# Weight buffers 128 bytes longer, and 41 weight panels written and read 32 or 64 bytes further on

## The reference

```python
for i in range(2):
    hn = rmsnorm(h, mix_norm[i])
    h = h + (mixer_ab if i == 0 else mixer_c)(hn, ...)
    u = rmsnorm(h, ffn_norm[i]) @ ffn_up[i]          # 1024 -> 2 x 2816
    gate, up = split(conv3(u) + conv_b)
    h = h + (silu(gate) * up) @ ffn_down[i]          # 2816 -> 1024
    h = h + sigmoid(rmsnorm(h, ple_norm[i]) @ ple_gate[i]) * (p[i] @ ple_proj[i])
```

## Time and profile before

| | |
|---|---|
| time, median of 3 runs | 1003.98 us (1003.67 to 1004.08) |
| time of the profiled execution | 1004.01 us |
| its span, first to last instruction | 1002.1 us |
| PE busy | 984.9 us, 98% |
| PEld busy | 883.2 us, 88% |
| DVE busy | 677.7 us, 68% |
| ACT busy | 573.5 us, 57% |
| granted TensorE clock | 1.000 |

### The profile page before, as it was taken

The page is one execution under the profiler, slowest core; times in us unless marked ns, Lnnn a source line. Parts: engine busy times, 40 slices in busy tenths (PEclk is TensorE's granted clock), DMA queues, the critical chain, the costliest instruction groups (busy, mean ns, idle before and its releaser), DMA issues.

```text
span 1002.1 us, 15515 instructions
## 1 busy us (share of the span) xinstructions
PE 984.9 (98%) x6218; PEld 883.2 (88%) x6218; DVE 677.7 (68%) x969; ACT 573.5 (57%) x801; POOL 133.8 (13%) x116
## 2 busy tenths in 40 slices
PE   8999999999999999999999999999999999999997
PEld 8998889999988888788999998888988889988886
DVE  5787577888864567886788886456564566854555
ACT  7747747656553576785756655356464465534433
POOL 4003202343310000000143331001000000000010
PEclk9999999999999999999999999999999999999999
DMA  9654256686555464336766655546635544466551
GB/s 310 207 170 126 84 146 178 197 250 195 185 195 184 167 210 168 126 103 171 198 172 182 194 172 203 177 166 205 211 127 169 168 149 146 142 197 205 175 172 56
DMA packets 159655, 174.33 MB, mean 174 GB/s; under 512 B 4126, under 2 KB 120336, under 8 KB 159584
## 3 DMA queue, kind: packets, MB, share of 16 engines
q1 hardware_dynamic: 157248, 167.65, 53.3%
q0 software_dynamic: 2160, 5.41, 1.7%
q10 hardware_dynamic: 176, 0.27, 0.1%
HBM read 172.25 MB, written 1.07 MB: 173 GB/s over the span
## 4 chain that ended last, share of the span: by engine, by line
PE 85%; ACT 6%; DVE 5%; issue 2%; DMA 1%; POOL 0%; POOLq 0%; ACTq 0%; DVEq 0%
PE bank L870 32%; PE bank L845 29%; PE bank L902 16%; PE bank L890 2%; ACT w_hi L1215 2%; PE bank L1004 1%; PE bank L930 1%; DVE w_lo L1541 1%; DMA w_raw<-in_ab_w_in 1%; ACT le L1325 1%; ACT L1325 1%; PE bank L950 0%; PE bank L973 0%; DVE le_s L1891 0%; ACT le_s L1465 0%
## 5 line engine op out<-in xcount | busy, mean ns | idle before, releaser
L1541 DVE TENSOR_TENSOR w_lo<-w_raw,w_hi 128x2048 fp32r<-128x2048 f32 x154 | 351.9, 2288 | 186.8 <-ACT w_hi L1215 186.6
L1215 ACT ACTIVATE w_hi<-w_raw 128x2048 fp32r<-128x2048 f32 x155 | 296.2, 1914 | 247.5 <-PE bank L870 114.2
L870 PE MATMUL bank<-x_hi,w_hi 128*128 128x256 f32 x720 | 205.9, 286 | 2.7 <-DVE w_lo L1541 1.8
L870 PE MATMUL bank<-x_lo,w_hi 128*128 128x256 f32 x720 | 203.7, 283 | 0.0
L870 PE MATMUL bank<-x_hi,w_lo 128*128 128x256 f32 x720 | 203.7, 283 | 0.0
L870 PEld LDWEIGHTS bank<-x_hi,w_hi 128*128 128x128 f32 x720 | 138.0, 192 | 4.4 <-DVE w_lo L1541 2.0
L845 PE MATMUL bank<-w_hi,x_hi 128*128 128x512 f32 x352 | 139.8, 397 | 1.0 <-DVE x_lo L1555 0.7
L870 PEld LDWEIGHTS bank<-x_lo,w_hi 128*128 128x128 f32 x720 | 138.1, 192 | 0.2
L870 PEld LDWEIGHTS bank<-x_hi,w_lo 128*128 128x128 f32 x720 | 138.0, 192 | 0.0
L845 PE MATMUL bank<-w_hi,x_lo 128*128 128x512 f32 x352 | 137.3, 390 | 0.0
L845 PE MATMUL bank<-w_lo,x_hi 128*128 128x512 f32 x352 | 137.1, 390 | 0.0
(11 more groups left out here) (344 smaller groups left out, 1471.6 us busy)
## 6 DMA issues: line engine op xcount, KB each, us to landing
w_raw<-in_ffn_up SPq DMA_DIRECT2D x88, 512.0 KB, 5.2
w_raw<-in_w_in SPq DMA_DIRECT2D x35, 1024.0 KB, 5.1
w_raw<-in_ffn_down SPq DMA_DIRECT2D x22, 1024.0 KB, 5.0
w_raw<-in_ab_w_in SPq DMA_DIRECT2D x13, 1024.0 KB, 5.4
w_raw<-in_ple_gate SPq DMA_DIRECT2D x8, 1024.0 KB, 5.1
w_raw<-in_c_w_in SPq DMA_DIRECT2D x6, 1024.0 KB, 5.3
w_raw<-in_ab_w_out SPq DMA_DIRECT2D x4, 1024.0 KB, 5.1
w_raw<-in_w_mem_kv SPq DMA_DIRECT2D x4, 1024.0 KB, 5.1
```

The lines of the kernel that those rows point to most:

```text
L870: mm = pe.matmul(bank[b][:, c * 256:c * 256 + 256], wv[w][:, k, c * P:(c + 1) * P], x[:, k, :], start=(k == 0 and m == 0 and not (first an ...
L1215: act.activation(whi[n % RING][:, :], raw[n % RAW][:, :], ACT.Copy).then_inc(*mark("weights_hi", ("hi", n)))
L1541: dve.tensor_tensor(wlo[n % RING][:, :], raw[n % RAW][:, :], plain(whi[n % RING][:, :]), ALU.subtract).then_inc(*mark("weights_lo", ("lo", ...
```

## The change

The six buffers of `w_hi` and `w_lo` become 32 floats (128 bytes) longer. In the panels of a table `SHIFTED`, the 2048 floats begin 8 or 16 floats (32 or 64 bytes) into the room instead of at its start; in the table the first number is for `w_hi`, the second for `w_lo`. The writers (ACT, DVE, POOL) and the reader (TensorE) all go by it. Everything behind a room moves by 128 bytes for each room ahead of it, `x_hi` and all that follows by 768 bytes. To make space, `causal` loses its own place and is loaded into columns 384 to 639 of `vecs`, which held the convolution's taps.

```diff
+SHIFT = 32
...
+SHIFTED = {}
+for _i in range(4):
+    SHIFTED["down0", _i], SHIFTED["down0", 4 + _i] = (16, 16), (0, 16)
+    SHIFTED["down1", _i], SHIFTED["down1", 4 + _i] = (16, 0), (8, 8)
+    SHIFTED["up1", 2 + _i], SHIFTED["up1", 7 + _i], SHIFTED["up1", 12 + _i], SHIFTED["up1", 17 + _i] = (16, 16), (0, 16), (16, 0), (8, 8)
+for _i in range(3):
+    SHIFTED["up0", 10 + _i], SHIFTED["up0", 14 + _i], SHIFTED["up0", 18 + _i] = (16, 16), (0, 16), (16, 0)
...
-        whi = [fixed(f"w_hi{i}", [P, 2048], F32R) for i in range(RING)]
-        wlo = [fixed(f"w_lo{i}", [P, 2048], F32R) for i in range(RING)]
+        hi_room = [fixed(f"w_hi{i}", [P, 2048 + SHIFT], F32R) for i in range(RING)]
+        lo_room = [fixed(f"w_lo{i}", [P, 2048 + SHIFT], F32R) for i in range(RING)]
+
+        def w_hi(n):
+            a = SHIFTED.get(PANELS[n][:2], (0, 0))[0]
+            return hi_room[n % RING][:, a:a + 2048]
+
+        def w_lo(n):
+            a = SHIFTED.get(PANELS[n][:2], (0, 0))[1]
+            return lo_room[n % RING][:, a:a + 2048]
...
-        causal = r("causal", [P, T])
...
+        causal = vflat[:, 3 * P:3 * P + T]
...
-                    load(causal[:, :], io["c_causal"], "causal")
+                    load(causal, io["c_causal"], "causal")
...
-                wh, wl = whi[n % RING], wlo[n % RING]
+                wh, wl = w_hi(n), w_lo(n)
```

More of the change, by code:

```diff
@@ L737, in _ @@
                     for c in (slice(512 * q, 512 * q + 512) for q in range(4)):
-                        pool.tensor_tensor(wlo[n % RING][:, c], raw[n % RAW][:, c], plain(whi[n % RING][:, c]), ALU.subtract).then_inc(*mark("weights_lo_p", ("lo", n)))
+                        pool.tensor_tensor(w_lo(n)[:, c], raw[n % RAW][:, c], plain(w_hi(n)[:, c]), ALU.subtract).then_inc(*mark("weights_lo_p", ("lo", n)))
                 elif kind == "sb_scores":
@@ L831, in panel @@
                     block, half = where[2:]
-                    wv = [w[:, :].rearrange("p (k n) -> p k n", k=4) for w in (wh, wl)]
+                    wv = [w.rearrange("p (k n) -> p k n", k=4) for w in (wh, wl)]
                     for t in range(TT):
@@ L855, in panel @@
                     claim(b, ("ev", n))
-                    wv = [w[:, :].rearrange("p (k n) -> p k n", k=KT) for w in (wh, wl)]
+                    wv = [w.rearrange("p (k n) -> p k n", k=KT) for w in (wh, wl)]
                     first = i == 0
@@ L883, in panel @@
                                 claim(out_bank(t, half), ("h", stage, t) if down else ("ym", stage[-1], 2 * t + half) if branch else ("ev", FIRST["gate" + stage[-1]] + 2 * half + 1))
-                    wv = [w[:, :].rearrange("p (k n) -> p k n", k=2) for w in (wh, wl)]
+                    wv = [w.rearrange("p (k n) -> p k n", k=2) for w in (wh, wl)]
                     if branch and last:
@@ L1214, in split @@
                         act.wait_ge(*at(("pe", n - RING)))
-                    act.activation(whi[n % RING][:, :], raw[n % RAW][:, :], ACT.Copy).then_inc(*mark("weights_hi", ("hi", n)))
+                    act.activation(w_hi(n), raw[n % RAW][:, :], ACT.Copy).then_inc(*mark("weights_hi", ("hi", n)))
             def split_piece(n, i):
@@ L1220, in split_piece @@
                 act.wait_ge(*at(("raw_half", i // 2) if n == 0 else ("raw", n)))
-                act.activation(whi[n % RING][:, c], raw[n % RAW][:, c], ACT.Copy).then_inc(*mark("weights_hi", ("hi_piece", n, i)))
+                act.activation(w_hi(n)[:, c], raw[n % RAW][:, c], ACT.Copy).then_inc(*mark("weights_hi", ("hi_piece", n, i)))
             act.dma_start(xn[0:2 * KT, 0, 0:P], io["mix_norm"].rearrange("l (a c) -> (l a) c", c=P)).then_inc(*mark("load_mix_gain", ("loaded", "mix_gain"), by=16))
@@ L1540, in split @@
                     dve.wait_ge(*at(("hi", n)))
-                    dve.tensor_tensor(wlo[n % RING][:, :], raw[n % RAW][:, :], plain(whi[n % RING][:, :]), ALU.subtract).then_inc(*mark("weights_lo", ("lo", n)))
+                    dve.tensor_tensor(w_lo(n), raw[n % RAW][:, :], plain(w_hi(n)), ALU.subtract).then_inc(*mark("weights_lo", ("lo", n)))
             def split_piece(n, i):
@@ L1546, in split_piece @@
                 dve.wait_ge(*at(("hi_piece", n, i)))
-                dve.tensor_tensor(wlo[n % RING][:, c], raw[n % RAW][:, c], plain(whi[n % RING][:, c]), ALU.subtract).then_inc(*mark("weights_lo", ("lo_piece", n, i), ("lo", n)))
+                dve.tensor_tensor(w_lo(n)[:, c], raw[n % RAW][:, c], plain(w_hi(n)[:, c]), ALU.subtract).then_inc(*mark("weights_lo", ("lo_piece", n, i), ("lo", n)))
             def rest(src, gain, hi, lo, name, event, *first):
```

## The result

The changed kernel takes 1008.97 us (median of 4 runs, 1008.27 to 1010.04) against 1003.97 us before (1003.67 to 1004.08): 5.0 us more, ratio 1.0048 with a 95% interval of 1.0036 to 1.0059. That is slower by more than 0.2% and inside the stated range of 1002.3 to 1012.5; the single forecast, 1005.9 us, was 3.1 us too low. The profiled execution took 1008.27 us, with a span of 1006.3 us, 4.2 us over the span before.

The account below looks back on a forecast made before the run. The prediction took PE's matmul pitch to bound the kernel. Its terms, 0.4 for `up1`, 1.3 for `up0` and 0.2 for `down`, summed to +1.9 us on 1003.98, giving 1005.9 us, with a stated range of 1002.3 to 1012.5.

Parts of the forecast that it names:

- no change that can be told: Outcome for the whole kernel: a time within 0.2%, 2.0 us of 1004; chance 0.48.
- the prediction's own signs: Profile signs of a wrong forecast: a pitch under 0.1178 in shifted panels, or other pitches by ring slot in unshifted ones.
- What bounds the kernel: PE, busy 98% of the span; in `up1`, `up0` and `down` matmul pitch goes to the end one for one.
- Longer buffers: Unshifted panels: rooms and inputs move apart by multiples of 128 bytes, no instruction added or removed; taken as 0.
- The 128 bytes matter: Rival: 128 bytes between operands act like 64, so unshifted panels change by ring slot; 1014 or 994 us, chance 0.12.
- `up1`: 16 shifted panels, weights stationary: equal pairs 0, eight unequal panels +0.05 us each, +0.4 together; ends -0.9 and +1.7.
- the short rhythm of `up0`: Pitch of 0.1178 us instead of 0.1200 in `up0`; as lower end for unequal `up1` pairs, -0.107 us a panel.
- `up0`, +1.3: Shifts from panel 10 on lose the short pitch in 12 panels, +1.3 us; ends 0 and +2.6.
- `down`, +0.2: 16 shifted panels, weights moving: equal pairs 0, eight unequal panels +0.03 us each; per-panel ends -0.053 and +0.105.
- The rival that a shifted stationary operand always costs: In `up1` and `up0` each shifted weight load costs 0.0131 us: +7.5 and +3.8 us, time 1015.3; chance 0.17.
- The working idea: Matmul stream and weight load lock in 128-byte steps; only successive operands lying differently matter, not where all lie.
- two pitches in `up0`: Argument against the skill's pages: `up0` shows 0.1200 and 0.1178 us for one instruction stream, so pitch depends on placement.

Follow-up runs that it names:

- rooms_only: The changed kernel with an empty table, so rooms 128 bytes longer and no panel shifted: 1009.93 us, ratio 1.0050 to the kernel before.
- empty_256: The changed kernel with rooms 256 bytes longer, `bsp` moved and an empty table, so no panel shifted: 1005.38 us in its one execution.
- table_256: The changed kernel with its table kept, rooms 256 instead of 128 bytes longer and `bsp` moved: 1005.26 us, ratio 1.0002 to the kernel before.
- y192: The changed kernel with rooms 256 bytes longer, no panel shifted and `y_lo` 192 bytes later: 1004.86 us.
- pair_all_f_y192: The changed kernel with rooms 256 bytes longer, `w_hi` 64 and `w_lo` 192 bytes off in all 67 F panels, `y_lo` 192 bytes later: 988.90 us, ratio 0.9842.

## Why the prediction was right in its range and wrong in its middle

**The range held by luck.** The terms that were named, +1.9 in the sum, measured -0.3 for the table's panels; the term that was put at 0 measured about +5 and made the result. Of the three outcomes "no change that can be told" had the best chance, 0.48, and "slower", which came, 0.41. By the prediction's own signs the forecast failed: there is a pitch under 0.1178 in shifted panels, and the unshifted ones differ by ring slot.

**What bounds the kernel.** Right: every change of pitch in the long stages came out at the end, and the waits of ACT on PE (38.7 us in 19 waits in `up1` after, 43.4 in 20 before) left room for the faster panels.

```profile
ACT w_hi L1233 <- PE bank L888: 38.7, 19, 2.4
```

**Longer buffers, taken as 0: the step that failed.** It was +5 to +6 us, the whole result, as `rooms_only` (ratio 1.0050) shows against `empty_256`. Half of it had been read correctly: a distance of 256 bytes does nothing. The sentence that 128 bytes were covered by no row was right, and its rival, "The 128 bytes matter", is what happened, with +5 where it had +10: in slot 1 the W panels lost only 0.003 us a matmul, and the F panels gained about 0.001.

**`up1`.** The sum had 0 for equal pairs, from the idea that only an unlike place of successive operands shifts the lock. Measured in `table_256`: -0.106 us a panel for (16,16), -0.08 for (8,8), and -0.106 for both unequal kinds, where +0.05 was taken between ends of -0.107 and +0.21. The lower end, the short rhythm of `up0`, was the answer for all. In the changed kernel (16,16) gave -0.31 a panel through the added 128 bytes, which no term had. The prediction held a pitch near 0.113 for very unlikely, because the first matmuls of `up1` fall back to 0.12; that row tells how one placement settles, and nothing of others.

**`up0`, +1.3.** That was for the twelve panels from 10 on. They measured +0.5 in the changed kernel, 0.2 of it in the nine shifted ones, and +0.1 in `table_256`. The rhythm was not lost for good by the shifts: only single panels ran slow (in `table_256` panel 17, at 0.1199).

**`down`, +0.2.** Measured +1.8 for the table's panels in both kernels, and in `table_256` +0.05 us a panel for (16,16), +0.12 for the unequal pairs, +0.16 for (8,8). The upper end of +0.105 from the earlier trace rows was the nearer row, and even it was too low.

**The table as a whole.** +1.9 forecast, -0.3 measured in the changed kernel (a difference of starts in one execution each) and no difference in `table_256`. Errors of both signs.

**The rival that a shifted stationary operand always costs** is refuted: in the changed kernel 15 of the 16 `up1` panels gained (panel 18, (8,8) in slot 1, cost 0.02 us), and in `table_256` all 16. **The working idea** survives in part. Several pitches fall on whole or half steps of 32 cycles over a group of three products: 0.1133 us is 816 cycles a group, 25.5 x 32; 0.1178 is 848; 0.1200 is 864; and for BT 0.2289 is 1648, 51.5 x 32. Others do not (0.1184, 0.1187, 0.1191 and 0.1209 us are 852 to 871 cycles), so the step is not shown to be a rule. Its grid of 128 bytes was wrong (256), and so was the conclusion that equal shifts are neutral. What in the memory makes the pitches stays open: the runs show places and pitches, not the reads.

The Trainium skill, "SBUF — State Buffer", section "Who interferes with whom", has PE waiting on nobody, and by "TensorE: Matmul & The Clock Gate", section "Step-by-step: what each phase is for", the weight load takes nothing from the moving operand. No trace here can tell whose read delays whose, but an effect of placement is certain: the matmuls of `up1` ran at 0.1133, 0.1178 or 0.1200 us each when only the places of their operands differed, and by these pages `rooms_only` would have cost nothing. The prediction's own argument against the pages, two pitches in `up0`, did not show this, as the placement there is one and the same; the rows that bore on it are those of W with input y and with input x.

## What to carry to other kernels

An edit that only makes a buffer longer moves everything behind it, and on a PE-bound kernel that alone can be worth half a per cent; look at the distances between matmul operands modulo 256 bytes, and keep padding in steps of 256 bytes unless another distance is meant. Where the weights are the stationary operand in hi/lo pairs with 256 columns moving, 64 and 192 bytes past the input was worth 5.6% of the pitch here, as long as both halves of the input were at one place modulo 256; with 512 columns moving, all operands at the same place was the best of the pairs tried. Measure pitch by stretch (length of an unbroken chain over its count) and sweep offsets panel by panel in one kernel: one run gives a dozen answers that whole-kernel times can't resolve.

## What was not expected of the hardware

- The pitch of float32r matmuls follows the distances of their SBUF operands, and distances that differ by 256 bytes act alike: for 128x128 weights and 256 columns 0.1133 to 0.1209 us, for 512 columns 0.2267 to 0.2335.
- Two steady pitches exist for one placement (0.1200 and 0.1178 in `up0` before), and a short break changes from one to the other; a `down` panel with (0,16) ran at 0.2317 or 0.2304 by what went ahead of it. With all operands at the same place modulo 256 there is only one (`y192`).
- In 5 of 13 profiled executions the granted clock falls to its lower level of 1.2 GHz in `qa`, during or just after a stretch without matmuls that every execution has there; in the other 8 it does not. The stretch lasted 1.9 to 3.5 us where it fell and 1.6 to 3.2 us where it did not, so its length does not decide. The windows of `pair_all_f_y192`, which was profiled in such an execution:

```profile
41.00:43.00 2.00, 0.00 (x0) 0.00 (x0) 2.00 (x1) 1.99 (x3) 0.00 (x0) 0.75 0.00 0
43.00:45.00 2.00, 1.80 (x8) 1.80 (x9) 2.00 (x3) 1.66 (x3) 0.00 (x0) 0.50 0.27 46
45.00:47.00 2.00, 2.00 (x12) 2.00 (x10) 2.00 (x5) 0.72 (x1) 0.00 (x0) 0.50 0.99 370
47.00:49.00 2.00, 2.00 (x12) 2.00 (x12) 0.88 (x3) 1.47 (x2) 0.00 (x0) 0.54 1.02 358
```
